# MLP down passes with weight sums made two passes ahead, totals copied first, two rows reloaded earlier, and the last pass's products in another order

## The reference, cut to what matters

```python
def sq_relu_mlp(h, w1, w2):
    return jnp.square(jax.nn.relu(h @ w1)) @ w2

        h = modulate(rmsnorm(x, norm_mlp_g[i]), sh2, sc2)
        x = x + g2[:, None, :] * sq_relu_mlp(h, mlp_w1[i], mlp_w2[i])
    return rmsnorm(x, final_g)
```

## Time and profile before

| | us |
|---|---|
| median of 3 runs | 2494.8 |
| profiled execution, own time | 2492.86 |
| its span | 2490.8 |
| PE busy | 2395.5 (96%) |
| DVE busy | 1699.9 (68%) |
| ACT busy | 1116.5 (45%) |
| POOL busy | 503.2 (20%) |

### The profile page before, as it was taken

How to read it: one execution, slowest core, us unless ns; L and a number is a source line. 1 busy time by engine, 2 the same in 40 slices (tenths; PEclk the granted TensorE clock), 3 DMA queues, 4 the chain that set the end, 5 groups by cost and what they waited for, 6 DMA issues and landing times.

```text
span 2490.8 us, 32717 instructions
## 1 busy us (share of the span) xinstructions
PE 2395.5 (96%) x11232; PEld 1943.3 (78%) x11232; DVE 1699.9 (68%) x2706; ACT 1116.5 (45%) x1946; POOL 503.2 (20%) x439
## 2 busy tenths in 40 slices
PE   7999999899998999999999899999999999999998
PEld 2578888688877888887888688878788897886677
DVE  7787877787777555267866677785651226998873
ACT  2355445444433223245555543342321226887850
POOL 0200001333333000200000333331010003557731
PEclk9899999899998999999999899999999999999999
DMA  8716655755435730434543764441444472336521
GB/s 310 270 56 210 225 204 195 265 166 164 135 101 165 223 104 18 150 112 156 186 169 131 256 197 135 153 131 34 152 139 133 148 188 73 87 98 171 159 68 68
DMA packets 272393, 380.13 MB, mean 153 GB/s; under 512 B 63601, under 2 KB 173297, under 8 KB 272241
## 3 DMA queue, kind: packets, MB, share of 16 engines
q1 hardware_dynamic: 272240, 378.17, 47.0%
HBM read 277.44 MB, written 106.69 MB: 154 GB/s over the span
## 4 chain that ended last, share of the span: by engine, by line
PE 85%; DVE 5%; POOL 3%; issue 3%; ACT 2%; DMA 2%; SPq 0%; POOLq 0%; DVEq 0%; ACTq 0%
PE banks L2696 22%; PE banks L2698 22%; PE banks L2697 22%; PE banks L3254 2%; PE banks L3272 2%; PE banks L2781 2%; DMA stage<-hidden 1%; POOL probs L1419 1%; PE banks L3039 1%; PE banks L3041 1%; PE banks L3040 1%; PE banks L3241 1%; PE banks L3242 1%; PE banks L2845 1%; PE banks L2737 1%
## 5 line engine op out<-in xcount | busy, mean ns | idle before, releaser
L2696 PE MATMUL banks<-Hhi,Whi 128*128 128x512 f32 x1760 | 700.1, 398 | 41.6 <-ACT UT L1638 12.9
L2697 PE MATMUL banks<-Hlo,Whi 128*128 128x512 f32 x1760 | 691.1, 393 | 0.0
L2698 PE MATMUL banks<-Hhi,Wlo 128*128 128x512 f32 x1760 | 691.0, 393 | 0.0
L2696 PEld LDWEIGHTS banks<-Hhi,Whi 128*128 128x128 f32 x1760 | 334.3, 190 | 121.3 <-issue 42.9
L2698 PEld LDWEIGHTS banks<-Hhi,Wlo 128*128 128x128 f32 x1760 | 334.0, 190 | 71.1
L2697 PEld LDWEIGHTS banks<-Hlo,Whi 128*128 128x128 f32 x1760 | 334.4, 190 | 70.6 <-issue 2.4
L2696 PE MATMUL banks<-T,Whi 128*128 128x512 f32 x720 | 281.5, 391 | 0.0
L2698 PE MATMUL banks<-T,Wlo 128*128 128x512 f32 x720 | 280.7, 390 | 0.0
L2697 PE MATMUL banks<-T,Whi 128*128 128x512 f32 x720 | 280.6, 390 | 0.0
L2373 DVE SCALAR_TENSOR_TENSOR X<-banks,mod,X 128x512 f32<-128x512 f32 x180 | 134.3, 746 | 94.2 <-PE banks L2698 93.8
L1419 POOL TENSOR_SCALAR probs<-probs,rden 128x1024 f32<-128x1024 f32 (+2 forms) x128 | 118.7, 928 | 336.8 <-DVE rden L2639 327.4
(11 more groups left out here) (259 smaller groups left out, 4196.4 us busy)
## 6 DMA issues: line engine op xcount, KB each, us to landing
stage<-w SPq DMA_DIRECT2D x58, 1024.0 KB, 6.9
stage<-hidden SPq DMA_DIRECT2D x224, 256.0 KB, 3.7
hidden<-slot SPq DMA_DIRECT2D x196, 256.0 KB, 2.1
stage<-ada_w SPq DMA_DIRECT2D x48, 1024.0 KB, 6.4
x_saved<-X SPq DMA_DIRECT2D x32, 512.0 KB, 4.1
stage<-w_in SPq DMA_DIRECT2D x13, 1024.0 KB, 6.3
X<-x_saved SPq DMA_DIRECT2D x24, 512.0 KB, 6.4
stage<-sgu_in SPq DMA_DIRECT2D x8, 1024.0 KB, 6.0
```

The lines of the kernel that those rows point to most:

```text
L2696: nc.tensor.matmul(out_bank, whi, xhi, start=start, stop=False, skip_group_check=onto)
L2697: nc.tensor.matmul(out_bank, whi, xlo, start=False, stop=False, skip_group_check=onto)
L2698: return nc.tensor.matmul(out_bank, wlo, xhi, start=False, stop=stop, skip_group_check=onto)
```

## The change

Six edits, all in the two MLPs:

1. `first_sums` moves from DVE to POOL, in its own right (p = 0 and p = 4).
2. POOL makes S1 and S3 of pass t + 2 during pass t, and S2 and S4 of pass t + 1. For this S4 is written into the weight block A11 in place of `S_sum`. The differences of the last chunk (`hidden_sum`) are made in pass 1, not in pass 0.
3. In pass 0 the two hidden tiles that stood ahead of everything stand behind product 0's weight copy, and the tiles of the next chunk start two products later. So the copy to `UT` has no tile of that chunk ahead of it.
4. Rows 0 and 1 of `X` are reloaded in `fast` p = 7, in place of p = 13.
5. The last pass runs its products in the order 1, 2, 3, 4, 5, 0, 6. Evictions, squares and the copy of the next weights move with it.
6. The statistics of half 0 come between product 0 and product 6 of that pass, and its spreading inside product 6. POOL adds ten tiles of squares in place of twelve after the first MLP, and TensorE makes two more sums of one tile.

```diff
+LAST_ORDER = (1, 2, 3, 4, 5, 0, 6)
-            steps[min(q + 2 * n, len(SIDES))].append((p, q))
+            steps[min(q + 2 * n + (2 if t == 0 else 0), len(SIDES))].append((p, q))
...
+SQUARED = {2: {(NPASS - 1, 1): (4, 5, 6, 7), (NPASS - 1, 2): (8, 9), (NPASS - 1, 3): (10,), (NPASS - 1, 4): (11, 12),
+               (NPASS - 1, 5): (13,), (NPASS - 1, 0): (14,)},
+           4: {(NPASS - 1, 1): (0, 1, 2, 3), (NPASS - 1, 2): (4, 5, 6, 7), (NPASS - 1, 3): (8,),
+               (NPASS - 1, 4): (9, 10, 11, 12), (NPASS - 1, 5): (13,), (NPASS - 1, 0): (14,)}}
...
@@ SP, fast
-                if last:
+                if p == PAIRS // 2:
                     sync.wait_ge(sums_lo, 16 * (l + 1))
...
                     reload_row(0)
                     reload_row(1)
+                if last:
                     sync.wait_ge(mod_done, T("mod"))
                     reload_row(2)
@@ POOL, pass_sums
-                            pool.wait_ge(ps_lo, 7 * n)
+                            pool.wait_ge(ps_lo, 7 * n - 4)
+                            pool.wait_ge(ps_sums, 4 * n)
...
-                        out, a, b, op = pass_columns(t, S_sum[:]), pass_block(T, t, 0, 1), pass_columns(t, S_sum[:]), ALU.subtract
+                        out, a, b, op = pass_block(T, t, 0, 0), pass_block(T, t, 0, 1), pass_columns(t, S_sum[:]), ALU.subtract
@@ POOL, fast and passes
+                if p == 0:
+                    first_sums(T, l, 0)
+                if p == 4:
+                    first_sums(T, l, 1)
...
                 if t + 1 < NPASS:
-                    pass_sums(T, l, t + 1, ("S1", "S3", "S2"))
-                    for n in range(4 if t == 0 else 0):
-                        hidden_sum(g, n)
-                    pass_sums(T, l, t + 1, ("S4",))
+                    pass_sums(T, l, t + 1, ("S2", "S4"))
+                for n in range(4 if t == 1 else 0):
+                    hidden_sum(g, n)
+                if t + 2 < NPASS:
+                    pass_sums(T, l, t + 2, ("S1", "S3"))
@@ ACT, passes
-                if t == 0:
-                    for p, q in right_steps(-1)[len(SIDES)]:
-                        right_hi(T, l, p, q)
-                for q in range(len(SIDES)):
-                    act.wait_ge(pass_done, 7 * (NPASS * l + t) + q + 1)
+                for q in order_of(t):
+                    act.wait_ge(pass_done, done_by(l, t, q))
                     if q == 1 and t == FIRST_PASS[o]:
+                        if t == 2:
+                            act.wait_ge(t_stored["T3"], 16 * PAIRS * (l + 1))
                         nc.scalar.activation(UT[:, o, :], fast_bank("A", t), ACT.Copy).then_inc(u_begun, 1)
                     if t + 1 < NPASS:
                         pass_hi(T, l, t + 1, base, q)
+                    if t == 0 and q == 0:
+                        for p, r in right_steps(-1)[len(SIDES)]:
+                            right_hi(T, l, p, r)
@@ DVE, fast
-                if p == 0:
-                    first_sums(T, l, 0, ("T1", "T3"))
-                elif not last:
+                if 0 < p and not last:
                     hidden_sum(g - 1, 0)
@@ PE
+            def block_stats(T, hf):
+
+                pe.wait_ge(sum_done, T("s", adds("blocks", 9 + 2 * hf)))
+                stat(T, hf, sums("blocks", hf), True, False, order="blocks")
+                for i in (12 + 2 * hf, 13 + 2 * hf):
+                    pe.wait_ge(sq_done, T("q", i + 1))
+                    stat(T, hf, sq_tile("blocks", i), False, i % 2 == 1, order="blocks")
...
+                        if t == NPASS - 1 and q == 6 and p == p0 + 1:
+                            spread(T, 0, B7)
                     ins.then_inc(pass_done, 1)
...
+                    if t == NPASS - 1 and then == 2 and q == 0:
+                        block_stats(T, 0)
```

More of the change, by code:

```diff
@@ L172, in raw_loads, with order_of, done_by @@
     return [[n for n in range(RAW + 6, 7 * CHUNKS) if max(place[n - RAW], 0) == t] for t in range(NPASS)]
+def order_of(t):
+    return LAST_ORDER if t == NPASS - 1 else range(len(SIDES))
+def done_by(l, t, q):
+    return 7 * (NPASS * l + t) + list(order_of(t)).index(q) + 1
 def evictions(t, q):
@@ L179, in evictions @@
     now = [] if name == "A1" and t == FIRST_PASS[o] else [(t, name)]
-    short = t > 0 and t - 1 in LAST_PASS and PASSES[t - 1][2] - PASSES[t - 1][1] < 3
-    if short and 1 <= q < 4:
+    if t == NPASS - 1:
+        return now + {1: [(t - 1, "U21")], 2: [(t - 1, "U22")], 3: [(t - 1, "U12"), (t, "U21")], 5: [(t, "U22")],
+                      0: [(t, "U12")]}.get(q, [])
+    if t - 1 == LAST_PASS[0] and 1 <= q < 4:
         now.append((t - 1, ("U22", "U21", "U12")[q - 1]))
-    if t in LAST_PASS and PASSES[t][2] - PASSES[t][1] > 2 and q > 3:
+    if t == LAST_PASS[2] and q > 3:
         now.append((t, ("U22", "U21", "U12")[q - 4]))
@@ L194 @@
 for _t in range(NPASS):
-    for _q in range(len(SIDES)):
+    for _q in order_of(_t):
         for _pair in evictions(_t, _q):
@@ L532, in summed @@
     def summed(order):
-        return KT - 2 if order == "pooled" else KT - 1
+        return KT - 2 if order in ("pooled", "blocks") else KT - 1
     def pooled_bank(n):
@@ L1149, in norm @@
                 if order == "blocks":
-                    sync.wait_ge(stat_done, T("st", 2 * KT if which == 4 else 4))
+                    sync.wait_ge(stat_done, T("st", 2 * KT if which == 4 else 6))
             def spatial(T):
@@ L1604, in norm @@
             def norm(T, which, order):
+                if order == "project":
+                    deviation(T, order, 0)
                 if order != "pooled":
-                    deviation(T, order, 0, which == 4)
                     deviation(T, order, 1, which == 4)
@@ L1648, in passes @@
                         nc.scalar.activation(Whi[:, T.n["w"] % 2, :], stage[:, s, :], ACT.Copy).then_inc(w_hi, 1)
-                for p, r in steps[len(SIDES)] if t >= 0 else ():
+                    if t == NPASS - 1 and q == 0:
+                        deviation(T, "blocks", 0, then == 4)
+                    for i in SQUARED[then].get((t, q), ()):
+                        block_square(T, l, i, then)
+                for p, r in steps[len(SIDES)]:
                     right_hi(T, l, p, r)
                 if t == NPASS - 1:
-                    for i in range(12, 16):
-                        block_square(T, l, i, then)
+                    block_square(T, l, 15, then)
             def block_square(T, l, i, then):
@@ L2178, in norm @@
                                             ALU.subtract).then_inc(gap_ready, 1)
-                invert(T, 0, which == 4)
+                if order != "blocks":
+                    invert(T, 0)
                 for n in range(2 * KT + 2):
@@ L2389, in passes @@
                         pass_lo(T, l, t + 1, base, q)
+                    if t == 0 and q == 0:
+                        for p, r in right_steps(-1)[len(SIDES)]:
+                            right_lower(T, l, p, r)
                     for p, r in steps[q]:
@@ L2395, in passes @@
                                                 Whi[:, T.n["w"] % 2, :].bitcast(F32), ALU.subtract).then_inc(unit_done, 1)
+                    if t == NPASS - 1 and q == 0:
+                        invert(T, 0, then == 4)
                 for p, r in steps[len(SIDES)]:
@@ L2818, in norm @@
                 if which == 4:
-                    for i in range(12, 2 * KT):
-                        both_stats(T, i)
+                    both_stats(T, 15)
                 elif order == "pooled":
@@ L2823, in norm @@
                 elif order == "blocks":
-                    for hf in range(NH):
-                        first_seven(T, order, hf)
-                        eighth(T, order, hf)
+                    block_stats(T, 1)
                 else:
@@ L2955, in passes @@
                 o, p0, p1 = PASSES[t]
-                for q, (_, side, bank, first) in enumerate(PRODUCTS):
+                for q in order_of(t):
+                    _, side, bank, first = PRODUCTS[q]
                     pe.wait_ge(ps_lo, 7 * n + q + 1)
```

82 lines of the change are left out of this document (37 added, 45 removed).

## The result

The changed kernel takes 2477.0 us (median of 4 runs, 2474.55 to 2480.28) beside 2495.9 for the kernel before: ratio 0.9926, 95% interval 0.9909 to 0.9943. The gain is 18.9 us where 37 were forecast, and the time lies 1 us above the range. The profiled execution's span is 2474.0 us, 16.8 less than before.

What follows compares the result with a forecast made beforehand. TensorE, busy 2395.5 of 2490.8 us, was taken to set the time, with only its waits and low clock recoverable. Gains of 7.4 + 16 + 5 + 6 + 2.5 = 36.9 us gave 2458 us, range 2446 to 2476.

Steps and rivals of the forecast that it cites:

- First sums: Up stage, p = 0: moving them to POOL shortens product 5's wait for the second join; 7.4 us gained over both MLPs.
- Order of the hidden differences: Hidden differences on POOL: moved work beside running matmuls, given no term of its own.
- Start of the down stage: Passes 0 and 1: tiles land 2.5 to 3.5 us sooner, product 4's wait shrinks; gains 8.5 and 7.5, together 16 us.
- Sums two passes ahead: Passes 14 and 16: S1 and S3 ready a pass earlier shorten the waits; 5 of 6.1 us gained.
- End of the first MLP: Last product to next stage: 9.7 us against 17.2, less 1.5 for a falling clock; 6 us gained.
- End of the second MLP: Pass 16 to next stage: chain of 5.6 us in place of 11.2 behind the last product; 2.5 us gained.
- 1.5 off: End of the second MLP: deduction in case four sums in one piece lower the clock, 4 us becoming 2.5.
- DVE takes over: Rival, chance 0.19: each POOL operation holds DVE for its full length; 21 us gained, 2474 us.
- a low clock in the last pass: Rival, chance 0.09: pieces of three and four sums let the clock fall; 26 us gained, 2469 us.
- The third: Rival, chance 0.08: chunk 3's first tile lands as late as before, so C1 still waits; 29 us gained, 2466 us.
- The fourth: Rival, chance 0.04: row reloads of X come late and stop DVE in pass 2; slower, 2502 us.

Runs made afterwards that it cites:

- e11: The changed kernel, but POOL makes the four differences of the last chunk in pass 0 again and not in pass 1: 2481.5 us, ratio 0.9948.
- e1: The changed kernel, but the four differences of chunk 2 (p = 4) are made by DVE again: 2474.0 us, ratio 0.9918.
- e2: The changed kernel, but all eight differences of the first two chunks are back on DVE: 2475.7 us, ratio 0.9931.
- e3: The changed kernel, but the second MLP's sums of squares are spread, one or two behind a product, in place of pieces of four: 2469.7 us, ratio 0.9902.

## Why the prediction was wrong

The gain was 20.2 us smaller by the stages than forecast, and 11.7 of them (6.9 in the up stages, 4.8 in p = 13) are one mistake in two places. The mechanism, an operation of POOL that stretches DVE's, was in the text and in a rival, but was priced only where the text looked, at p = 0, and nowhere else POOL's work had moved. Of another kind are the landings at the start of the down stage and the clock at the end of the second MLP.

- *First sums.* The step "the differences of chunk 2 at the end of p = 4 cost nothing now and nothing later; PE has no wait there" failed. They did cost nothing on DVE, behind its last step of p = 4; on POOL they run as soon as their inputs are ready, 31 us earlier in p = 3, beside the work for the second join: 5.9 us over both MLPs. For chunk 1 the size was near: product 5 of p = 0 waits 1.25 us at a clock of 1.00, where the earlier trace rows had 3.06, and 5.6 us came where 7.4 were forecast.
- *Order of the hidden differences.* "Moved work beside running matmuls; no term of its own" failed: p = 13 lost 4.8 us (4.2 in the mean of eleven traces), and pass 0 without the four differences gained 6.2 (e11).
- *Start of the down stage.* 11.2 for 16: 4.0 for 8.5 in the first MLP, 7.2 for 7.5 in the second; in e1, e2 and e3, which share the stage, 5.2 to 5.8 and 5.2 to 6.2. The step that failed: "I put the landings behind them 2.5 to 3.5 us sooner", and with it a tile that "lands near 450", 7.2 us behind the start of pass 0. In the first MLP ACT took it up at 455.2 us, 10.6 behind that start, where it was 10.1 before, and in the mean of the twelve traces 9.1. In the second MLP the gain was as forecast, 8.0 behind the start where it was 11.5, but that is still later than 7.2, and DVE's rest of the tile took 1.28 us beside POOL. So C1 was 3.7 us late in both and not 2, and pass 1 waited 1.1 and 1.4.
- *Sums two passes ahead.* 3.3 for 5, within the bounds: product 5 still waits about 1 us in passes 14 and 16.
- *End of the first MLP.* 8.9 for 6 (6.5 to 8.9 over the sixteen traces, mean 7.8): the 1.5 us taken off for a falling clock were not needed, the granted clock from 745 to 766 us is 1.00. The chain came out as worked: from the end of product 6 at about 765.7 us 4.6 us to the next stage, forecast 4.7. The changed kernel, PE, which answers to the earlier trace rows:

```profile
765.50 0.95 PE L2762 MATMUL banks<-ones,UT 128*128 128x1 f32 x8
766.31 1.96 PE L2762 MATMUL banks<-ones,stage 128*128 128x1 f32 x16
768.98 1.13 PE L2800 MATMUL banks<-const,rstd 128*128 128x128 f32 x8 [0.71 <-DVE rstd L2081]
770.29 0.77 PE L3075 MATMUL banks<-Whi,Hhi 128*128 128x512 f32 x1 [0.18 <-DVE Hlo L2210]
```

- *End of the second MLP.* A loss of 1.4 (3.2 in the mean of eleven traces) for a gain of 2.5. The term "1.5 off" for pieces of four sums was mis-sized: they cost 7.6 us (e3). The chain behind the last product was right, 5.4 us for 5.6.

Of the rivals the first, DVE takes over, came nearest: 2474 us for 2477. It had the ends at 4 and 1 and the start at 10; what it lacked was p = 3 and p = 13, since it counted POOL's operations only at p = 0. That its time is near is luck in part: its 10 us at the start of the down stage were 11.2, its 3.6 for the first sums came to nothing, and its 4 and 1 at the ends were 8.9 and a loss of 1.4. The second, a low clock in the last pass, was right for the second MLP and wrong for the first. The third, the copy to `UT` no longer waits but C1 does, describes pass 0 best: 4 us per MLP forecast, 4.0 and 7.2 measured. The fourth did not come: PE has no wait in pass 2.

## What to carry to other kernels

Before work moves to another engine, list every DVE operation with two SBUF inputs in the window in which the moved work will run, which is when its inputs are ready and not where it stood; each costs up to the length of the one beside it. Read a changed trace by the shift of the same instruction from stage to stage: sums of the whole hide losses such as those of p = 3 and p = 13, and differences of medians do too. And where a late engine has two causes in a row, test them together, since each alone looks worthless.
